# A float32 transformer pair on one core: the residual adds and the operand splits at three hand-overs, rearranged

## What is computed

```
merged = sigmoid(gate_a) * (y_attn @ w_attn_branch) + sigmoid(gate_b) * (y_hgrn @ w_hgrn_branch)
x = x + rms_norm(merged @ w_out, g_mix_post)
h = rms_norm(x, g_ffn_pre); gate, up = split(h @ w_gate_up)
x = x + rms_norm((silu(gate) * up) @ w_down, g_ffn_post)
x = x + rms_norm((p @ w_ple_proj) * sigmoid(rms_norm(x) @ w_ple_gate), g_ple_post)
```

```
h = layernorm(x) * (1 + scale) + shift
p = h @ w_in[l]            # u, z, cq, ckv, k_r, z_a
...
x = layernorm(ALPHA * x + gate * (y @ w_out[l]))
```

## Time and profile before

| | |
|---|---|
| median of 3 runs | 2232.94 us (2231.92 to 2234.74) |
| profiled execution, its own time | 2233.09 us |
| its span, first to last instruction | 2231.2 us |
| mean granted TensorE clock | 0.996 of full |
| PE busy | 2194.5 us (98%) |
| DVE busy | 1513.4 us (68%) |
| ACT busy | 1110.8 us (50%) |
| POOL busy | 46.0 us (2%) |
| HBM traffic | 224 GB/s over the span |

### The profile page before, as it was taken

The page is one execution under the profiler, slowest core; times in us unless marked ns, Lnnn a source line. Parts: engine busy times, 40 slices in busy tenths (PEclk is TensorE's granted clock), DMA queues, the critical chain, the costliest instruction groups (busy, mean ns, idle before and its releaser), DMA issues.

```text
span 2231.2 us, 26898 instructions
## 1 busy us (share of the span) xinstructions
PE 2194.5 (98%) x10449; PEld 1832.1 (82%) x10449; DVE 1513.4 (68%) x1967; ACT 1110.8 (50%) x1516; POOL 46.0 (2%) x68
## 2 busy tenths in 40 slices
PE   9999999999999999999999999998999999999997
PEld 7888888888888888888888888887888887788886
DVE  6675468768876777777777778766465566555566
ACT  6575456444445444444433444565465454546542
POOL 1000000100000000000000000000000000000000
PEclk9999999999999999999999999999999999999999
DMA  7544655499795889998989988573464582554573
GB/s 260 186 127 129 186 179 163 143 373 309 262 331 188 297 298 308 307 308 302 304 302 306 311 301 299 181 238 95 142 194 137 161 279 81 165 166 147 159 234 117
DMA packets 242607, 500.61 MB, mean 224 GB/s; under 512 B 17008, under 2 KB 26144, under 8 KB 241328
## 3 DMA queue, kind: packets, MB, share of 16 engines
q1 hardware_dynamic: 239088, 484.08, 66.4%
q0 software_dynamic: 3392, 14.82, 1.9%
HBM read 496.70 MB, written 2.12 MB: 224 GB/s over the span
## 4 chain that ended last, share of the span: by engine, by line
PE 91%; DVE 3%; ACT 3%; issue 1%; DMA 1%; POOL 0%; SPq 0%; POOLq 0%; ACTq 0%; DVEq 0%
PE bank L898 88%; PE bank L901 3%; DVE wl L1866 1%; ACT arena L1312 1%; ACT wh L1312 1%; DMA raw<-in_w_in 1%; DVE arena L1874 0%; DVE arena L1873 0%; DVE arena L1869 0%; DMA raw<-in_w_ple_gate 0%; ACT hh L1312 0%; DVE arena L1866 0%; ACT L1312 0%; DVE hl L1866 0%; POOL st L749 0%
## 5 line engine op out<-in xcount | busy, mean ns | idle before, releaser
L1312 ACT ACTIVATE wh<-raw 128x1024 fp32r<-128x1024 f32 (+2 forms) x500 | 520.0, 1042 | 664.3 <-PE bank L898 621.6
L1866 DVE TENSOR_TENSOR wl<-raw,wh 128x1024 fp32r<-128x1024 f32 (+2 forms) x500 | 599.5, 1201 | 325.6 <-ACT wh L1312 323.6
L898 PE MATMUL bank<-wh,hh 128*128 128x512 f32 (+1 forms) x1568 | 619.9, 396 | 9.4 <-DVE hl L1866 5.2
L898 PE MATMUL bank<-wl,hh 128*128 128x512 f32 (+1 forms) x1568 | 605.5, 387 | 0.0
L898 PE MATMUL bank<-wh,hl 128*128 128x512 f32 (+1 forms) x1568 | 605.3, 387 | 0.0
L898 PE MATMUL bank<-wh,ah 128*128 128x512 f32 (+1 forms) x1168 | 456.1, 391 | 2.4 <-ACT arena L1312 1.7
L898 PE MATMUL bank<-wh,al 128*128 128x512 f32 (+1 forms) x1168 | 450.9, 387 | 0.0
L898 PE MATMUL bank<-wl,ah 128*128 128x512 f32 (+1 forms) x1168 | 450.2, 386 | 0.0
L898 PEld LDWEIGHTS bank<-wh,hh 128*128 128x128 f32 x1568 | 295.4, 189 | 69.0 <-issue 9.8
L898 PEld LDWEIGHTS bank<-wh,hl 128*128 128x128 f32 x1568 | 294.5, 188 | 60.6
L898 PEld LDWEIGHTS bank<-wl,hh 128*128 128x128 f32 x1568 | 296.0, 189 | 55.3
(11 more groups left out here) (132 smaller groups left out, 1356.5 us busy)
## 6 DMA issues: line engine op xcount, KB each, us to landing
raw<-in_w_in SPq DMA_DIRECT2D x245, 512.0 KB, 3.7
arena<-in_w_ada SPq DMA_DIRECT2D x148, 384.0 KB, 4.9
arena<-in_w_gate_up SPq DMA_DIRECT2D x97, 512.0 KB, 4.5
raw<-in_w_ada SPq DMA_DIRECT2D x108, 384.0 KB, 4.8
raw<-in_w_out SPq DMA_DIRECT2D x80, 512.0 KB, 5.0
raw<-in_w_gate_up SPq DMA_DIRECT2D x79, 512.0 KB, 4.6
raw<-in_w_down SPq DMA_DIRECT2D x45, 512.0 KB, 5.2
arena<-in_w_down SPq DMA_DIRECT2D x43, 512.0 KB, 5.2
```

The lines of the kernel that those rows point to most:

```text
L898: return i.matmul(o, l, x, start=start, stop=stop, skip_group_check=False)
L1312: return i.activation(o, x, fn, scale=scale, **k)
L1866: return i.tensor_tensor(o, a, b, op)
```

## The change

Two parts. First, in the merged branches, the sums, the root and the residual adds are done by token half. Behind the first half of the last block, `wo_half` closes m = 0 (sum, mean, gain row, root on POOL for one column), and in the next two slots DVE adds the first 512, the second 512 and the third 512 columns of m = 0. At the feed-forward's first slot `wo_end` closes m = 1, and `res_add` adds m = 1 alone for n = 0, 1 and 2, and both for n = 3. `close("Y2")` is gone.

Second, pairs 2 to 7 of a layer's operand are three entries instead of one: `h_turn` (PE's transposes, one slot earlier than before), `h_affine` (the float32 values on DVE and ACT, in the slot before the pair's old one, but behind that slot's weight tiles, through the new table `BEHIND`), and `h_split` (ACT's copy and DVE's subtraction, at the pair's old slot). `norm(l, 2)` moves from slot 2 to slot 1 and `norm(l, 3)` from slot 4 to slot 3. Pairs 0 and 1 stay, and so does `keep`.

```diff
@@ timetable
     ahead(f, "wo_end")
     ahead(f, "keep", 30, "ffn")
-    ahead(f, "close", "Y2", "")
...
-        for t, name, n in ((0, "norm", 0), (0, "norm", 1), (0, "h_pair", 0), (0, "h_pair", 1), (1, "h_pair", 2), (2, "norm", 2),
-                           (2, "h_pair", 3), (3, "h_pair", 4), (4, "norm", 3), (4, "h_pair", 5), (5, "h_pair", 6), (6, "h_pair", 7)):
+        for t, name, n in ((0, "norm", 0), (0, "norm", 1), (0, "h_pair", 0), (0, "h_pair", 1), (1, "norm", 2), (3, "norm", 3)):
             ahead(f + t, name, l, n)
+        for p in range(2, 8):
+            ahead(f + p - 2, "h_turn", l, p)
+            behind(f + p - 2, "h_affine", l, p)
+            ahead(f + p - 1, "h_split", l, p)
@@ drive
                 if LEAN <= t < NS and eng == "dve":
                     main(t)
+                for name, args in BEHIND.get(t, ()):
+                    if name in stages:
+                        stages[name](*args)
@@ pool
+            def wo_root(m):
+                e.wait_ge(*S.v_rms.at("wo", m))
+                root(RSTD[:, m:m + 1], SSUM[:, m:m + 1], 1, S.g_rms.up("wo", m))
+
+            def wo_half():
+                wo_root(0)
+                yield
+
+            def wo_end():
+                wo_root(1)
@@ act (copy of pair p >= 2; the affine part is a function of its own)
+            def h_affine(l, p):
+                ph, T = f"H5{l}", TT2[p % 2].rearrange("p (k t) -> p k t", k=2)
+                scale, bias = h_columns(l, p)
+                e.wait_ge(*S.p_op.at(ph, p))
+                e.wait_ge(*S.v_op.at(ph, p - 2))
+                f(T[:, 1, :], BANK[bank_of[ph, p, 1]][:, 0:256], ACTF.Identity, scale=scale[1], bias=bias[1]).then_inc(*S.a_aff.up(l, p))
+
+            def h_split(l, p):
+                ph, T = f"H5{l}", TT2[p % 2].rearrange("p (k t) -> p k t", k=2)
+                e.wait_ge(*S.a_aff.at(l, p))
+                e.wait_ge(*S.v_aff.at(l, p))
+                h_free(ph, p)
+                copy(pair_of(ph, p)[0], T).then_inc(*S.a_op.up(ph, p))
@@ dve
+            def wo_root(m):
+                o = SSUM[:, m:m + 1]
+                e.wait_ge(*S.a_sq.at("wo", 3, m))
+                then(red(o, SS[:, m:m + 1, :], ALU.add), S.v_rms, "wo", m, 0)
+                ts(o, o, 1.0 / D, EPS, ALU.mult, ALU.add).then_inc(*S.v_rms.up("wo", m))
+                then(wo_row(3, m), S.v_ev if m else S.v_evh, INDEX["wo", 3])
+
+            def wo_add(n, m):
+                cs = slice(n * 512, (n + 1) * 512)
+                e.wait_ge(*S.get(f"d_xr{n}").at())
+                e.wait_ge(*S.g_rms.at("wo", m))
+                return stt(XR[:, m, cs], YR[:, m, cs], RSTD[:, m:m + 1], XR[:, m, cs], ALU.mult, ALU.add)
+
             def wo_half():
-                wo_row(3, 0).then_inc(*S.v_evh.up(INDEX["wo", 3]))
-                yield
+                wo_root(0)
+                yield
+                wo_add(0, 0)
+                wo_add(1, 0)
+                yield
+                wo_add(2, 0)
...
+            def h_low(l, p):
+                ph = f"H5{l}"
+                hi, lo = pair_of(ph, p)
+                e.wait_ge(*S.v_aff.at(l, p))
                 e.wait_ge(*S.a_op.at(ph, p))
-                tt(lo, T, hi.bitcast(F32), ALU.subtract).then_inc(*S.v_op.up(ph, p))
+                tt(lo, TT2[p % 2].rearrange("p (k t) -> p k t", k=2), hi.bitcast(F32), ALU.subtract).then_inc(*S.v_op.up(ph, p))
...
+            def h_affine(l, p):
+                e.wait_ge(*S.p_opa.at(f"H5{l}", p))
+                affine(l, p, BANK[bank_of[f"H5{l}", p, 0]][:, 0:256], 0).then_inc(*S.v_aff.up(l, p))
+
+            def h_split(l, p):
+                h_low(l, p)
```

More of the change, by code:

```diff
@@ L367, in wait_ge @@
             self.seen[id(sem)] = v
-AHEAD, START = {}, {}
+AHEAD, START, BEHIND = {}, {}, {}
 LEAN = 10
@@ L377, in ahead, with behind @@
     AHEAD.setdefault(t, []).append((name, args))
+def behind(t, name, *args):
+    BEHIND.setdefault(t, []).append((name, args))
 def start(t, name, *args):
@@ L876, in pool @@
             drive("pool", lambda t: None, dict(
-                xstats=xstats, lb=lb, hgrn=hgrn, wa=wa, wh=wh, close=close, after=after, pn=pn, prefetch=prefetch,
+                xstats=xstats, lb=lb, hgrn=hgrn, wa=wa, wh=wh, wo_half=wo_half, wo_end=wo_end, close=close, after=after, pn=pn,
+                prefetch=prefetch,
                 pg_half=pg_half, pg_a=pg_a, pre=pre, fourier=fourier, cq=cq, ckv=ckv, gate_row=gate_row, ln_rows=ln_rows,
@@ L1671, in norm, with h_columns, h_free @@
                   bias=NM[:, 0:1]).then_inc(*S.a_norm.up(l, n))
+            def h_columns(l, p):
+                k = 48 * l + 2 * p
+                return [MOD[:, k + 16 + z:k + 17 + z] for z in range(2)], [MOD[:, k + z:k + z + 1] for z in range(2)]
+            def h_free(ph, p):
+                if before(ph, p) is not None:
+                    e.wait_ge(*S.p_unit.at(before(ph, p)))
             def h_pair(l, p):
                 ph = f"H5{l}"
-                hi = pair_of(ph, p)[0]
+                hi, (scale, bias) = pair_of(ph, p)[0], h_columns(l, p)
@@ L1676, in h_pair @@
                 e.wait_ge(*S.p_op.at(ph, p))
[L1677 to L1681, removed]
-                e.wait_ge(*S.v_mod.at(l, "s"))
[L1683 to L1693, removed]
+                h_free(ph, p)
@@ L1855, in act @@
                 res_pair=res_pair, after=after, gate=gate, up=up, down=down, pn_t=pn_t, pproj=pproj, pgate=pgate,
-                pg_half=pg_half, pg_a=pg_a, pg_b=pg_b, mix=mix, norm=norm, h_pair=h_pair, u=u, fourier=fourier, cq=cq,
+                pg_half=pg_half, pg_a=pg_a, pg_b=pg_b, mix=mix, norm=norm, h_pair=h_pair, h_affine=h_affine, h_split=h_split, u=u, fourier=fourier, cq=cq,
                 ckv=ckv, zf=zf, za=za, qb=qb, kvb=kvb, mla=mla, gate_row=gate_row, wo2=wo2, ln_half=ln_half, ln_a=ln_a,
@@ L2242, in res_add @@
                 if ph == "Y2":
-                    e.wait_ge(*S.get(f"d_xr{n}").at())
+                    if n == 3:
+                        wo_add(n, 0)
+                    wo_add(n, 1).then_inc(*S.v_res.up(ph, n))
+                    return
                 for m in range(2):
@@ L2559, in dve @@
                 res_pair=res_pair, after=after, up=up, down=down, pn_t=pn_t, pgate=pgate, pg_a=pg_a, pg_b=pg_b,
-                pg_half=pg_half, pre=pre, norm=norm, h_pair=h_pair, u=u, fourier=fourier, cq=cq, ckv=ckv, zf=zf, za=za, qb=qb,
+                pg_half=pg_half, pre=pre, norm=norm, h_pair=h_pair, h_affine=h_affine, h_split=h_split, u=u, fourier=fourier, cq=cq, ckv=ckv, zf=zf, za=za, qb=qb,
                 mla=mla, wo2=wo2, ln_half=ln_half, ln_a=ln_a, ln_b=ln_b))
```

48 lines of the change are left out of this document (24 added, 24 removed).

## The result

| | before | after |
|---|---|---|
| median of the runs compared (18 each) | 2232.03 us (2231.35 to 2234.74) | 2229.3 us (2227.66 to 2231.92) |
| after/before | | 0.9986, 95% interval 0.998 to 0.9992 |
| profiled execution: its own time, its span | 2233.09, 2231.2 | 2228.5, 2226.7 |
| granted clock, mean | 0.996 | 0.997 |
| PE's waits for the low part of a layer's operand | 5.2 us, 6 times | 5.3 us, 7 times |

The change makes the kernel 2.7 us faster. The interval is 1.8 to 4.5 us, so the gain is real, though smaller than the 0.2% that I called the limit of this measurement. Forecast were 2230.4 us and a gain of 2.67.

The account below looks back on a forecast made before the run. TensorE, busy 98% of the span, bounds the kernel, so only PE's waits can be won. Gains of 0.22 + 0.90 + 1.55 = 2.67 us from 2233.09 give 2230.4 us; range 2227.2 to 2233.6.

Parts of the forecast that it names:

- the gain is at most 680.41 - 680.19 = 0.22 us: Merged branches: the filler stays in front, so the first transposes gain only PE's 0.22 us of idling behind it.
- from slot 0 on ... they are worth nothing: Feed-forward from slot 0: DVE has three adds of 0.70 us less, worth nothing as PE ran without a gap.
- my outer bound of 0.71: Merged branches: 0.71 us less between root and transposes, the most to gain if the filler didn't stand in front.
- 0.90 forecast: Layer 0: norm 2 and 3 each replace 0.45 us of DVE's wait for the copy; unit 7 0.90 us earlier.
- The sign that I named against C: Layer 0: unit 1 to unit 7 takes 21.7 us; staying at 22.6 would mean C.
- C: Rival: hardly anything gained; another wait takes the norms' 0.45 us back and the filler covers the merged half; 2232.8 us, chance 0.16.
- 0.65 for the transposes: Layer 1: earlier transposes end DVE's 0.48 us wait at pair 2 and ACT's 0.17 us lateness; gain 0.65 us.
- The unchanged cycle: Pairs 2 to 7: DVE's order stays value, wait for the copy, subtraction, tile, still idling 0.83 us while ACT copies.
- B: Rival: DVE's loop really broken, its round 2.56 us, below PE's 3.19; gain 8.0 us, 2225.1 us, chance 0.12.
- My objection that the tile's place would tie unit t+2 to unit t: Layers, against B: even with the loop broken, unit t itself gives back the tile's place, tying unit t+2 to it.
- the rule of the Trainium skill that I weighed: DVE's next instruction waits for an empty pipeline; each norm then worth 0.54 us, 2230.1 us; forecast kept 0.45.
- D: Rival: slower; the granted clock falls in units 5 to 7 of both layers; 2233.8 to 2235.4 us, chance 0.08.

Follow-up runs that it names:

- c1: The changed kernel run again unaltered, 11 runs beside 15 of the kernel before; median 2228.75 us, ratio 0.9985.
- e7: The changed kernel with the first token half's root still early but its three adds back in the feed-forward's slots; 2229.13 us, single run.
- e1: The changed kernel with norm 2 and norm 3 behind the slot's weight tile, just ahead of h_affine; 2238.38 us, single run.
- e2: The changed kernel with each h_turn behind its slot's unit instead of ahead of it, norms as in the change; 2231.73 us, single run.
- e9: The changed kernel with only DVE's part of norm 2 and norm 3 moved behind the slot's subtraction; 2230.19 us, single run.
- e3: The kernel before with the merged branches' part of the change alone, layers as before; 2231.35 us, single run.
- e4: The changed kernel with h_affine ahead of the slot's weight tile instead of behind it; median 2224.42 us, 0.9952 of the kernel before.
- e10: The changed kernel with h_affine ahead of the tile, 26 feed-forward filler transposes instead of 30, and 76 and 116 before the layers, not 58 and 82; 2221.05 us.
- e6: The kernel before with the layers' part of the change alone, merged branches as before; 2230.16 us, single run.
- e5: The changed kernel with 26 filler transposes instead of 30 ahead of the feed-forward's first pairs; 2228.3 us, single run.

## Why the prediction came out right, and which terms were off

The kind of change in each place was forecast rightly, and the total was met more closely than its terms. 0.22 + 0.90 + 1.55 = 2.67 was forecast, 0.61 + 0.95 + 1.75 = 3.31 measured in the traces, and 2.7 (or 3.3, beside `c1`) between medians. That 2.67 and 2.7 agree to a few hundredths is luck.

**Merged branches: right in kind, mis-sized.** The step "the gain is at most 680.41 - 680.19 = 0.22 us" took the filler's modelled end for the point at which the next transposes can start. In the changed kernel they start 3.27 us behind its start, not 3.44 (matmuls overlap in PE). That makes it 0.39 at the transposes and 0.45 at unit 0. The step "from slot 0 on ... they are worth nothing" was wrong by 0.17: `e7` shows the second pair of adds holding pair 2's transposes. Together 0.61, near my outer bound of 0.71. Root, adds and tiles moved as worked out: one-column roots of 0.56 and 0.58 us, at the lower of the two prices. The last half's reduction, for which I had 0.1 to 0.5 us of lateness, wasn't late.

**Layer 0: right.** 0.90 forecast, 0.95 measured. The rounds show it: the one with a `norm` and one tile was 3.84 before and is 3.39 after, `e1` brings one back to 3.84, and `e2` shows that the early transposes carry nothing here. `e9` gives back only 0.37 of it, as its `norm` stands partly in another wait. The sign that I named against C failed all the same: unit 1 to unit 7 was to take 21.7 us and took 22.95. I had held unit 1 fixed, while its start hangs on how fast unit 0 runs and unit 7's does not.

**Layer 1: right to 0.2 us, and partly by luck.** 1.55 forecast, 1.75 measured (1.61 in `c1`). I added 0.90 for the `norm`s and 0.65 for the transposes, and done together they came as added: 0.90, 0.67, and 0.16 more ahead of the loop. `e2` shows that the `norm`s' part needs the transposes': without them the first `norm` would have cost time on ACT, which my sum didn't say. The 0.65 also hangs on the clock at the layer's start, which differs between executions of the same order. `e3` has the old order, and there the first eight transposes took 1.73 us instead of 1.97, pair 2's value stood at 19.71 without any wait for transposes, and unit 7 at 42.04 instead of 42.95: the 0.65 wasn't there to be won. The four transposes ahead of unit 0, which I had as a delay of 0.4 to 0.6 us for units 0 to 2 in layer 1, delayed none: unit 0 is at 15.65 in both kernels, and units 1 and 2 come 0.93 earlier.

**The unchanged cycle.** This was the reading on which the forecast stood against B, and it holds: six waits of DVE for the copy in layer 0, 4.1 us in all where before there were 5.0, four at 0.83 and two at 0.37. B's own arithmetic holds as well, as `e4` makes what the change does not: 33.94 instead of 38.12. My objection that the tile's place would tie unit t+2 to unit t was right as a description, and cost PE 0.2 us in layer 0.

**The DRAIN.** DVE's next instruction starts 0.46 us behind the value's start at 1536.19, which lasts 0.54. By the rule of the Trainium skill that I weighed ("VectorE: DVE Perf Modes", section "The DRAIN you can't avoid") each `norm` would be worth 0.54; the trace disagrees again, `e1`'s round being 0.45 longer. The same section of the Trainium skill goes on that a next instruction that is not held starts earlier. I had weighed only its first half; with the second the trace agrees (0.46 behind an instruction of 0.54).

**C and D.** C fell with the layers' 2.7 us, counted from the fillers. D asked for a clock that falls between units 1 and 7. It stayed at 1.00, in the stretches of the changed kernel (columns as in the earlier trace rows):

```profile
1534.00:1557.00 23.00, 20.13 (x90) 15.05 (x90) 17.28 (x23) 13.87 (x20) 0.00 (x0) 1.00 0.55 164
1885.00:1907.00 22.00, 19.74 (x93) 15.31 (x91) 16.97 (x22) 13.62 (x20) 0.00 (x0) 1.00 0.59 172
```

## What to carry to other kernels

Where two in-order engines hand a value back and forth, write out one round of each, and check whether an edit changes the order around the wait or only moves the whole round: here an added step in the wait was free, and an instruction moved across the tile took the wait away and gained 5.4 us in the two layers' traces, twice what the change had gained there. Before moving work into or out of a wait, look for who needs its result: in `e1` the `norm` behind the tile held up PE's transposes and cost 5.6 us where its own price was 0.9. A filler's price is read from where the next instruction starts, and lengthening it up to the point at which the real work is ready pays only where the clock would fall otherwise (0.8 us in layer 1, nothing in layer 0). Measure a stage from a point that the change can't move to the point that sets what follows, here from the filler to unit 7, and not between two points that both move.

## What was unexpected of the hardware

**The clock at a layer's start is not a property of the code.** PE idles 2.36 or 2.37 us ahead of layer 0's first transposes in every run but `e10`. The stretch from 1530 to 1533 us, in the changed kernel with the last of the first transposes and most of unit 0, then in `e6`, whose layers are the same, with the first transposes and the start of unit 0:

```profile
1530.00:1533.00 3.00, 2.67 (x14) 2.07 (x13) 2.32 (x5) 3.00 (x6) 0.00 (x0) 1.00 0.00 0
```

```profile
1530.00:1533.00 3.00, 2.65 (x13) 2.66 (x14) 0.93 (x3) 2.50 (x6) 0.00 (x0) 0.54 0.00 0
```

Of five traces with these layers, two had unit 1 at 14.22 (the changed kernel and `c1`, granted clock 1.00 in this stretch) and three at 14.93, 15.00 and 15.05 (`e6`, `e5`, `e7`, granted clock 0.54 or 0.55). `e6` reached unit 1 at 14.93 instead of 14.22 and unit 7 0.46 later: what delays PE alone is covered, as DVE sets the pace from unit 2 on, but what delays DVE's first value isn't. In `e5` and `e7` that value came at 16.15 and 16.16, and unit 7 at 37.19 and 37.20. Two single profiles can differ by this much in a stage without a cause in its code. What decides it isn't shown. After the 4.2 us of idling ahead of layer 1 the first transposes were slowed in every run that had them (12 took 1.73 to 2.82 us, against the 1.53 of `e10`). In `e1` the granted clock was still 1.00 after a wait of 2.35 us, and 0.65 in the stretch of the one of 2.97.

**The filler's transposes hold the clock.** In `e10` PE runs nothing but them between 1866 and 1875 us, at a granted clock of 1.00, one each 0.11 us. The Trainium skill says in "TensorE: Matmul & The Clock Gate", section "Part 4: PE-mode transpose", that in this mode the high clock doesn't engage, as it doesn't count as TensorE work in the same way. The trace disagrees, at least for keeping a clock that is already up.
